# Feed-forward stage of a fused transformer kernel: four seven-product pairs in place of three, with half of their weight sums on GpSimd

## What is computed

```python
D_MODEL = 1024; SEQ = 256; DEPTH = 4; D_FF = 2816

def swiglu(x, w13, w2):
    gate, up = jnp.split(x @ w13, 2, axis=-1)
    return (jax.nn.silu(gate) * up) @ w2

for i in range(DEPTH):
    x = layer_norm(ALPHA * x + 0.5 * swiglu(x, ffn1_w13[i], ffn1_w2[i]), ln_g[i, 0], ln_b[i, 0])
    ...
    x = layer_norm(ALPHA * x + 0.5 * swiglu(x, ffn2_w13[i], ffn2_w2[i]), ln_g[i, 2], ln_b[i, 2])
```

## Time and profile before

| | us |
|---|---|
| median of 3 runs | 2465.51 (2463.6 to 2465.53) |
| the profiled execution, its own time | 2466.14 |
| its span, first to last instruction | 2464.2 |
| PE busy | 2410.9 (98% of the span), 13023 matmuls |
| DVE busy | 1852.3 (75%) |
| ACT busy | 1319.6 (54%) |
| POOL busy | 409.4 (17%) |
| largest total wait of PE by one cause | 5.8 |

### The profile page before, as it was taken

The page is one execution under the profiler, slowest core; times in us unless marked ns, Lnnn a source line. Parts: engine busy times, 40 slices in busy tenths (PEclk is TensorE's granted clock), DMA queues, the critical chain, the costliest instruction groups (busy, mean ns, idle before and its releaser), DMA issues. The chain is left out here.

```text
span 2464.2 us, 32871 instructions
## 1 busy us (share of the span) xinstructions
PE 2410.9 (98%) x13023; PEld 2027.1 (82%) x13023; DVE 1852.3 (75%) x2384; ACT 1319.6 (54%) x1637; POOL 409.4 (17%) x463
## 2 busy tenths in 40 slices
PE   9999999999999999999989999999999998999999
PEld 7888878888888888888878888888878876998998
DVE  5466679889875798898768888887675667897554
ACT  5444555555664556556556655664553355444442
POOL 0002310000001100000230000001359602580000
PEclk9999999999999999999999999999999999999999
DMA  8555445656554465565515565565445542336553
GB/s 273 188 187 156 143 146 190 204 171 200 193 172 137 137 197 196 177 199 188 167 58 184 188 209 171 187 206 158 133 149 191 189 153 71 116 124 205 171 188 111
DMA packets 313945, 418.10 MB, mean 170 GB/s; under 512 B 18761, under 2 KB 271042, under 8 KB 313794
## 3 DMA queue, kind: packets, MB, share of 16 engines
q1 hardware_dynamic: 313794, 416.01, 51.8%
HBM read 414.92 MB, written 1.05 MB: 169 GB/s over the span
## 5 line engine op out<-in xcount | busy, mean ns | idle before, releaser
L536 DVE TENSOR_TENSOR wlo<-raw,whi 128x2048 fp32r<-128x2048 f32 (+1 forms) x370 | 861.4, 2341 | 159.0 <-ACT whi L529 158.2
L529 ACT ACTIVATE whi<-raw 128x2048 fp32r<-128x2048 f32 (+1 forms) x375 | 700.4, 1887 | 6.0 <-DMA raw<-in_ffn_w_dram 3.1
L695 PE MATMUL ps<-whi,xh 128*128 128x512 f32 (+2 forms) x1367 | 510.8, 374 | 7.9 <-DVE wlo L1647 2.2
L697 PE MATMUL ps<-whi,xl 128*128 128x512 f32 (+2 forms) x1367 | 503.5, 368 | 0.0
L696 PE MATMUL ps<-wlo,xh 128*128 128x512 f32 (+2 forms) x1367 | 503.1, 368 | 0.0
L695 PE MATMUL ps<-whi,oh 128*128 128x512 f32 x944 | 380.1, 403 | 0.0
L697 PE MATMUL ps<-whi,ol 128*128 128x512 f32 x944 | 369.0, 391 | 0.0
L696 PE MATMUL ps<-wlo,oh 128*128 128x512 f32 x944 | 367.9, 390 | 0.0
L695 PEld LDWEIGHTS ps<-whi,xh 128*128 128x128 f32 x1367 | 258.0, 189 | 56.8 <-issue 11.9
L697 PEld LDWEIGHTS ps<-whi,xl 128*128 128x128 f32 x1367 | 257.9, 189 | 43.2
L696 PEld LDWEIGHTS ps<-wlo,xh 128*128 128x128 f32 x1367 | 258.2, 189 | 41.0
(11 more groups left out here) (412 smaller groups left out, 3988.8 us busy)
## 6 DMA issues: line engine op xcount, KB each, us to landing
raw<-in_ffn_w_dram SPq DMA_DIRECT2D x350, 512.0 KB, 4.9
raw<-in_ffn_w_dram SPq DMA_DIRECT2D x88, 1024.0 KB, 5.0
raw<-in_w_ff_dram SPq DMA_DIRECT2D x32, 1024.0 KB, 5.4
raw<-in_w_out_dram SPq DMA_DIRECT2D x20, 1024.0 KB, 4.9
raw<-in_w_in_dram SPq DMA_DIRECT2D x20, 1024.0 KB, 5.1
raw<-in_dsa_w_in_dram SPq DMA_DIRECT2D x32, 512.0 KB, 4.6
raw<-in_dsa_w_in_dram SPq DMA_DIRECT2D x12, 1024.0 KB, 5.1
raw<-in_fox_w_in_dram SPq DMA_DIRECT2D x16, 512.0 KB, 5.0
```

The lines of the kernel that those rows point to most:

```text
L529: act.activation(hi(u)[:, 0:w], raw[:, (slot[u] + 1) % SLOTS, 0:w], ACT.Copy).then_inc(sem("hi_ready"), n)
L536: dve.tensor_tensor(lo(u)[:, 0:w], raw[:, (slot[u] + 1) % SLOTS, 0:w], hi(u)[:, 0:w].bitcast(F32), ALU.subtract).then_inc(sem("lo_ready"), n)
L695: pe.matmul(o, ah, bh, start=start, stop=False, skip_group_check=True)
L697: return pe.matmul(o, al, bh, start=False, stop=stop, skip_group_check=True)
```

## The change

Pairs now begin at columns 3, 5, 7 and 9, so four pairs follow each other with no plain column between. Sums 3 and 4 of every pair are made by POOL; sum 4 goes to a tile of its own. Where another pair follows, DVE and ACT make what `before_pair` did at the end of `paired`: sum 1 ahead of the first gated remainder, then the low part of unit v+6, sum 2 and so on. At the end of the last pair the second remainder (`gated_low(q + 1)`) now stands ahead of the low part of the second of the units that follow.

```diff
-PAIRED = (3, 6, 9)
+PAIRED = (3, 5, 7, 9)
...
+                if kind == "ffn":
+                    A, D = ffn_units(st)
+                    for n, q in enumerate(st["pairs"]):
+                        v = A(q + 1)
+                        landed(pool, v + 1)
+                        landed(pool, v + 2)
+                        pool.wait_ge(sem("form_made"), b("form_made", 0) + 2 * n + 1)
+                        pool.tensor_tensor(raw_of(v + 1), raw_of(v + 2), raw_of(v + 1), ALU.add).then_inc(sem("third_form"), 1)
+                        landed(pool, v + 3)
+                        pool.wait_ge(sem("form_made"), b("form_made", 0) + 2 * n + 2)
+                        pool.wait_ge(sem("form_hi"), b("form_hi", 0) + 4 * n + 1)
+                        if n:
+                            pool.wait_ge(sem("form_used"), b("form_used", 0) + 3 * n)
+                        pool.tensor_tensor(form_4[:, :], raw_of(v + 3), form_2[:, :], ALU.add).then_inc(sem("fourth_form"), 1)
...
@@ ACT, the end of paired(q) @@
+                        if q + 2 in pairs:
+                            split_hi(act, v + 6)
+                            gated_high(q)
+                            form_high(n + 1, 1, form_1h, form_1)
+                            form_high(n + 1, 2, form_2h, form_2)
+                            gated_high(q + 1)
+                            return
...
@@ DVE, the start of paired(q) @@
-                        tt(raw_of(v + 1), raw_of(v + 2), raw_of(v + 1), ALU.add).then_inc(sem("form_made"), 1)
+                        dve.wait_ge(sem("third_form"), b("third_form", 0) + n + 1)
                         split_lo(dve, v + 2)
-                        landed(dve, v + 3)
-                        tt(form_2[:, :], raw_of(v + 3), form_2[:, :], ALU.add).then_inc(sem("form_made"), 1)
                         form_low(n, 3, lo(v + 1), raw_of(v + 1), hi(v + 1))
+                        dve.wait_ge(sem("fourth_form"), b("fourth_form", 0) + n + 1)
                         split_lo(dve, v + 3)
-                        form_low(n, 4, form_4l, form_2, form_4h)
+                        form_low(n, 4, form_4l, form_4, form_4h)
...
@@ DVE, the end of paired(q) @@
+                        if q + 2 in pairs:
+                            two_summed(q + 2)
+                            gated_low(q)
+                            three_summed(q + 2)
+                            form_low(n + 1, 1, form_1l, form_1, form_1h)
+                            gated_low(q + 1)
+                            form_low(n + 1, 2, form_2l, form_2, form_2h)
+                            return
                         gated_low(q)
+                        split_lo(dve, v + 6)
+                        gated_low(q + 1)
                         split_lo(dve, v + 7)
-                        gated_low(q + 1)
-                        split_lo(dve, v + 8)
```

More of the change, by code:

```diff
@@ L175, in stages_plan @@
             n = len(st["pairs"])
-            made.update(h0_done=FIT - 2 * n, rows_made=min(n, 1), rows_hi=min(n, 1), rows_lo=min(n, 1), form_made=4 * n, form_hi=4 * n,
+            made.update(h0_done=FIT - 2 * n, rows_made=min(n, 1), rows_hi=min(n, 1), rows_lo=min(n, 1), form_made=2 * n, third_form=n, fourth_form=n, form_hi=4 * n,
                         form_lo=4 * n, form_used=3 * n, third_done=n, term_kept=4 * n, block_made=3 * n)
@@ L360, in build @@
         form_2 = nc.alloc_sbuf_tensor_at("form_2", [P, W], F32, offset=heads_at + 8 * W)
-        form_4l = nc.alloc_sbuf_tensor_at("form_4l", [P, W], F32R, offset=heads_at + 8 * W)
+        form_4h = nc.alloc_sbuf_tensor_at("form_4h", [P, W], F32R, offset=heads_at + 8 * W)
         form_2h = nc.alloc_sbuf_tensor_at("form_2h", [P, W], F32R, offset=heads_at + 12 * W)
         form_2l = nc.alloc_sbuf_tensor_at("form_2l", [P, W], F32R, offset=cx_at)
-        form_4h = nc.alloc_sbuf_tensor_at("form_4h", [P, W], F32R, offset=xT_at)
+        form_4 = nc.alloc_sbuf_tensor_at("form_4", [P, W], F32, offset=xT_at)
+        form_4l = nc.alloc_sbuf_tensor_at("form_4l", [P, W], F32R, offset=xT_at)
         rows_s = nc.alloc_sbuf_tensor_at("rows_s", [P, 4, 4, P], F32, offset=xn_at)
@@ L1091, in form_high @@
                     def form_high(n, f, dst, src):
-                        act.wait_ge(sem("form_made"), b("form_made", 0) + 4 * n + f)
+                        if f == 3:
+                            act.wait_ge(sem("third_form"), b("third_form", 0) + n + 1)
+                        elif f == 4:
+                            act.wait_ge(sem("fourth_form"), b("fourth_form", 0) + n + 1)
+                            act.wait_ge(sem("form_lo"), b("form_lo", 0) + 4 * n + 2)
+                        else:
+                            act.wait_ge(sem("form_made"), b("form_made", 0) + 2 * n + f)
                         act.activation(dst[:, :], src[:, :], ACT.Copy).then_inc(sem("form_hi"), 1)
@@ L1111, in paired @@
                         keep(n, 2, 5)
-                        form_high(n, 4, form_4h, form_2)
+                        form_high(n, 4, form_4h, form_4)
                         split_hi(act, v + 4)
@@ L1790, in row_lows, with two_summed @@
                         tt(rows_l[:, :, :, :], rows_s[:, :, :, :], rows_h[:, :, :, :].bitcast(F32), ALU.subtract).then_inc(sem("rows_lo"), 1)
-                    def before_pair(q):
-                        n, v, made = pairs.index(q), A(q + 1), b("form_made", 0) + 4 * pairs.index(q)
+                    def two_summed(q):
+                        v = A(q + 1)
                         landed(dve, v)
@@ L1797, in before_pair, with three_summed @@
                         tt(form_1[:, :], raw_of(v + 1), raw_of(v), ALU.add).then_inc(sem("form_made"), 1)
+                    def three_summed(q):
+                        n, v = pairs.index(q), A(q + 1)
                         split_lo(dve, v)
                         landed(dve, v + 2)
-                        dve.wait_ge(sem("form_made"), made + 1)
+                        dve.wait_ge(sem("form_made"), b("form_made", 0) + 2 * n + 1)
                         tt(form_2[:, :], raw_of(v + 2), form_1[:, :], ALU.add).then_inc(sem("form_made"), 1)
+                    def before_pair(q):
+                        n = pairs.index(q)
+                        two_summed(q)
+                        three_summed(q)
                         gate_rows(q - 1, 0, ps[:, 4, 256:512])
```

## The result

| | before | after the change |
|---|---|---|
| time, median of the runs (us) | 2465.52 (4 runs, 2463.6 to 2466.55) | 2663.19 (4 runs, 2660.01 to 2664.43) |
| ratio, 95% interval | 1 | 1.0801 (1.0789 to 1.0813) |
| the profiled execution, own time / span (us) | 2466.14 / 2464.2 | 2664.43 / 2662.6 |
| mean granted clock | 0.996 | 0.972 |

The change costs 197.7 us. The forecast was 2654, with a range of 2600 to 2695: the time is 9 us above it and inside the range.

A forecast was written before the change was run, and what follows sets the result against it. PE was taken to bound the kernel, with DVE close behind. From 2465.5 us, waits less savings added 153 and the lowered clock 35: 2654 us, range 2600 to 2695, chance 0.84.

The forecast's parts named there:

- Saved, 20.8 us: Six feed-forward stages: 12 fewer matmuls each, 16.3 us in all, plus six last-column waits for the second remainder gone, 4.5 us.
- POOL's addition: One 128x2048 sum on POOL: 4.6 us, extrapolated from smaller additions, bounds 2.4 and 9.0 us.
- The exclusion: POOL and DVE instructions reading SBUF shut each other out for whole instructions: DVE spared 2.2 us per sum, blocked up to 4.6.
- The first wait: Before each stage's first pair, PE waits 7.1 us for DVE's second gate, delayed by POOL's sum 4.
- From pair to pair: Three times a stage, PE waits 1.2, 0.4, 1.7 and 4.0 us for DVE, 7.3 us together.
- The lap: Time from one pair to the next: PE's 31.1 us plus 7.3 of waits, 38.4 us, with DVE the bound.
- Sum without the clock: Waits less savings over six stages, at full PE clock: +153 us on 2465.5.
- The clock: PE falls to 1.2 GHz after long waits: 35 us, 16 after first waits and about 19 after 18 others; bounds 0 and 62.
- Rival 1: No exclusion between POOL and DVE; PE keeps only 18 waits of 1.2 us for the moved remainder: 2466 us, chance 0.06.
- Rival 2: No exclusion, and the moved remainder also comes in time for PE: 2445 us, chance 0.04.
- Rival 3: POOL starts later or holds DVE more briefly, so half the collisions occur: 2538 us, chance 0.06.
- what was to be seen: Trace signs: 48 POOL additions of 4.5 us or more, DVE busy near 1852 or rising, PE waits of 7 and 4 us.

The follow-up runs named there:

- Experiment 3: Kernel before the change, with only the last pair's second remainder moved ahead of the second unit's low part: 2461.6 us, ratio 0.9983.
- experiment 1: Changed kernel with all four sums of each pair on DVE and none on POOL: 2504.69 us, ratio 1.0156.
- experiment 5: Changed kernel with each of POOL's 128x2048 additions cut into four of 128x512: 2570.41 us, ratio 1.0433.
- experiment 7: Changed kernel with all sums on DVE, and POOL only filling sum 4's tile with zeros where it made sum 3: 2504.47 us, ratio 1.016.
- experiment 8: Changed kernel with all sums on DVE, and POOL adding a tile to itself, result unused, where it made sum 3: 2565.4 us, ratio 1.0411.
- experiment 4: Changed kernel with unused matmuls keeping PE busy through its two long waits (before a stage's first pair, and for `form_2l`): 2617.36 us, ratio 1.0612.

## Why the prediction was right

**Saved, 20.8 us.** The 72 matmuls are gone from the count. Experiment 3 measured the early remainder by itself at 4.3 us, against 4.5. The 16.3 of the matmuls were not run alone; experiment 1's account (60 - 20.8 = 39.2, measured 38.8) agrees with them.

**POOL's addition.** Estimated at 4.6 us from two shorter ones; measured 4.60 for sum 3 (median of 24) and 4.51 for sum 4 in the first pair, where it starts free.

**The exclusion**, read from one collision on tiles half as long, is right. In the prediction's walk DVE's sum 2 ends at 384.3, the first gate at 384.6 and the second at 391.7; the trace has 384.45, 384.78 and 391.58. The first wait is 6.68 us for the predicted 7.1. The Trainium skill's rule (SBUF — State Buffer, section "Who interferes with whom") had been cited for this; experiments 5, 7 and 8 agree with it, quarter by quarter and for a fill against an addition.

**From pair to pair.** Predicted 1.2, 0.4, 1.7 and 4.0 us; measured, start to start, 1.25, 0.26, 1.56 and 3.66. The sum is 6.7 for 7.3. The lap was given as 38.4; with the clock kept up it is 38.33 (experiment 4). So the lap is longer than PE's 31.1 by somewhat more than the four waits. Most of the last 0.5 is in the first matmul after each wait: in experiment 4 the next one starts 0.31 to 0.34 us after it in place of 0.23, four times in a lap.

**Sum without the clock.** Predicted 2465.5 + 153 = 2619; experiment 4 measured 2617.4.

**The clock is the term that was off:** 35 us, measured 45.8. I had 16 for the six first waits and 19 for the 18 others, on the ground that DVE sets the lap and covers part of what PE loses. The rows say otherwise. Counting in PE's timeline the 128x512 matmuls that take 0.55 us or more after each of these waits: all 24 waits are followed by some. After the six waits for the gate there are 5 to 9 (47 in all), after the 18 for `form_2l` 7 to 13 (174 in all). Each starts 0.20 us later than at full clock, so these are 221 x 0.20 = 44 us, and 0.4 us for each first turn makes 47. By this count the first waits cost 2.0 us each, less than the 2.6 taken, and the others 1.9 each, twice what I had. The total is what experiment 4 measured, so next to nothing was covered.

Why nothing was covered can be read from the starts of DVE's sum 1 and of PE's first matmul with `form_2h`, where the 3.5 us wait ends:

| lap | matmuls at half clock | sum 1 to `form_2h` | `form_2h` to next sum 1 | lap (us) |
|---|---|---|---|---|
| changed kernel, from 419.73 | 13 | 20.25 | 20.74 | 40.99 |
| changed kernel, from 637.42 | 7 | 20.27 | 19.51 | 39.78 |
| experiment 4, from 454.71 | 0 | 20.30 | 18.02 | 38.33 |
| experiment 5, from 411.34 | 0 | 15.85 | 22.04 | 37.88 |
| experiment 5, from 611.59 | 8 | 16.14 | 21.72 | 37.86 |

All 18 times that a pair follows a pair in the changed kernel the first part is 20.25 to 20.28 us: that is DVE's queue with POOL's holds in it. The second goes through PE. Its last gates read products that PE has yet to make, and without a fall it takes 18.02, about what it takes after a first pair's `form_2h` (17.91), where PE never waits. So "DVE sets the lap" was half the truth: DVE and PE set it in turn, and the clock fell in PE's part, where each late matmul makes the lap later. In experiment 5 the clock falls in DVE's part, PE's part is no longer the bound (22.0 against 18.0), and a fall costs nothing.

Together: -20.8, + 6 x 6.7, + 18 x 7.2, + 45.8 gives +195, measured +197.7.

**The rivals.** Rivals 1 and 2 (no exclusion) fall by the 6.4 us rows beside experiment 7's 2.28. Rival 3 (POOL comes too late for half the collisions) falls by the rows of L906 and L912: in the pair shown POOL starts 0.18 us after sum 1's end (422.01) and 0.14 after sum 2's (431.13), as assumed, and the medians of 4.60 and 6.52 over 24 pairs say that it goes so in each stage. Of what was to be seen, one item was put badly: DVE's busy time was to stay "near 1852 or rises". It rose by 186 us. A held instruction counts as busy: with all sums on DVE it was busy for 1953.5 (experiment 1's page), 48 additions of 2.2 less are 1848, and the 190 above that are 4.0 us for each of POOL's 48 additions.

**Open:** why the half clock lasts 12 or 13 matmuls after some waits and 7 or 8 after others of the same 3.5 us. It isn't random: in each of the last five stages the first two waits for `form_2l` have 7 or 8 and the third 12 or 13, while the first stage has 13 each time. Nor is it known why in experiment 5 seven of 18 waits of the same 2.04 to 2.13 us are followed by a fall and eleven are not. No run here varied either.

## What to carry to other kernels

Before moving an elementwise instruction from DVE to POOL, compare what DVE is spared (2.2 us here) with how long POOL's instruction shuts it out (4.5 us here), and look for a DVE instruction with two SBUF inputs that will stand beside it; where there always is one, the move costs even though POOL is idle. If it must be moved, try short pieces: here DVE's held time fell from 190 to 128 us (DVE busy for 1976.2 us less the same 1848), the long waits of PE went and with them what the clock cost, and the instruction that PE needs first came sooner. It was still 66 us slower than leaving the sums on DVE (2570.4 against 2504.7). To price a fall of the clock, ask whether PE or another engine sets the pace in the stretch right after it. And split a change with several parts: the small reordering at the end of each stage was worth 4 us alone and was buried under 200.

## What the runs showed of the hardware that was not expected

- Cutting POOL's additions into quarters doubles POOL's busy time in a lap (22.3 us against 11.1) and gives back 93 us of 198, with a lap only 0.45 us shorter.
- PE's clock fell after each of the 24 waits of 3.5 to 6.5 us, and in the kernel with quarters after seven of 18 waits of 2.04 to 2.13 us. In the changed kernel a wait of 3.5 us costs 1.4 to 2.7 us more than itself; in the kernel with quarters a fall lengthened no lap (37.86 to 37.91 us with one, 37.87 to 37.90 without).
- Extra matmuls with no use made the kernel 45.8 us faster.
- POOL's addition of 128x2048 takes 3.60 us when both inputs are one tile, against 4.51 to 4.60 with two; its fill of the same size takes 1.81 and holds nobody.
